# Hybrid decoder step: key steps of the samples moved from the prompt's attention into the projections

## The reference, cut to what matters

```
h = rmsnorm(x);  p = h @ w_in            -> q, k (4 heads x 2 components x 64), v (4 heads x 128), conv input
prompt:  a = softmax(q0.k0) - lam * softmax(q1.k1), causal over 512 keys;  o = a @ v
sample:  the same over 4096 cached keys and the new one;                   o = a @ cached v
x = x + concat(rmsnorm(o), swish(layernorm(causal depthwise conv, 31 taps))) @ w_out
x = x + MoE(rmsnorm(x))                  32 experts, top 4, clamped SwiGLU
```

## Time and profile before

| | |
|---|---|
| median of 3 runs | 1733.65 us (1730.45 to 1736.07) |
| the profiled execution's own time | 1735.41 us |
| its span (first to last instruction) | 1733.7 us |
| busy: PE / DVE / ACT / POOL | 1474.0 / 782.4 / 356.0 / 96.7 us |
| mean granted TensorE clock | 0.903 of full speed |
| DMA | 598.10 MB, mean 345 GB/s |

### The profile page before, as it was taken

The page is one execution under the profiler, slowest core; times in us unless marked ns, Lnnn a source line. Parts: engine busy times, 40 slices in busy tenths (PEclk is TensorE's granted clock), DMA queues, the critical chain, the costliest instruction groups (busy, mean ns, idle before and its releaser), DMA issues.

```text
span 1733.7 us, 32093 instructions
## 1 busy us (share of the span) xinstructions
PE 1474.0 (85%) x11950; PEld 595.0 (34%) x11951; DVE 782.4 (45%) x1160; ACT 356.0 (21%) x822; POOL 96.7 (6%) x173
## 2 busy tenths in 40 slices
PE   3868887779788978899998998999899999899970
PEld 2433333346433354332332332333233332232320
DVE  2789879997786335221332232132132131131326
ACT  3212212222222111111211211212112122121220
POOL 0000010000000000000100000000000000000000
PEclk8989995679898857999999999999899999999995
DMA  9557888988998785598999999999999999999986
GB/s 327 182 187 258 283 295 272 331 279 292 311 301 270 242 352 207 227 392 339 429 420 403 427 417 396 412 418 411 392 421 412 401 428 411 397 428 399 428 351 253
DMA packets 127292, 598.10 MB, mean 345 GB/s; under 512 B 20503, under 2 KB 20517, under 8 KB 102026
## 3 DMA queue, kind: packets, MB, share of 16 engines
q1 hardware_dynamic: 109088, 560.20, 81.9%
q10 hardware_dynamic: 8634, 20.00, 3.4%
q0 software_dynamic: 9504, 17.06, 2.6%
HBM read 589.36 MB, written 25.87 MB: 355 GB/s over the span
## 4 chain that ended last, share of the span: by engine, by line
PE 40%; DMA 19%; DVE 2%; issue 1%; ACT 0%; DVEq 0%; SPq 0%; ACTq 0%
PE bank L1511 25%; DMA wts<-in_w_gate_up 16%; PE bank L1548 8%; PE bank L1530 4%; DMA wts<-in_w_down 3%; PE bank L1501 1%; PE bank L1618 1%; DVE v_ring L2139 1%; PE bank L1559 1%; PE bank L1599 0%; DVE q_b L2139 0%; DMA h_tok<-h_rows,v_tok 0%; ACT k_T L1155 0%; DVEq L2127 0%; ACT k_T L1138 0%
## 5 line engine op out<-in xcount | busy, mean ns | idle before, releaser
L1511 PE MATMUL bank<-wts,h_T 128*32 128x512 f32 x4032 | 443.9, 597 | 9.7 <-DMA wts<-in_w_gate_up 5.2
L2061 DVE TENSOR_SCALAR q_T<-bank 128x512 f32<-128x512 f32 x32 | 22.1, 692 | 636.9 <-PE bank L1511 636.9
L1511 PEld LDWEIGHTS bank<-wts,h_T 128*32 128x32 f32 x4032 | 129.5, 111 | 308.3 <-issue 296.4
L1548 PE MATMUL bank<-wts,k_T 128*32 128x512 f32 x2048 | 228.3, 597 | 8.0 <-issue 4.9
L1530 PE MATMUL bank<-wts,h_T 128*32 128x512 f32 x992 | 132.6, 675 | 52.2 <-DMA wts<-in_w_gate_up 50.4
L1658 DVE TENSOR_TENSOR wts<-wts,q_b 128x1024 f32<-128x1024 f32 x128 | 158.1, 1235 | 23.1 <-DMA wts<-in_cache_k 17.4
L1661 DVE TENSOR_REDUCE sc<-wts 128x16 f32<-128x1024 f32 x128 | 156.2, 1220 | 4.4
L1145 ACT ACTIVATE h_T<-bank 128x512 f32<-128x512 f32 x66 | 35.9, 595 | 573.5 <-PE bank L1501 573.5
L1548 PEld LDWEIGHTS bank<-wts,k_T 128*32 128x32 f32 x2048 | 64.9, 110 | 149.0 <-issue 139.5
L1223 PE MATMUL bank<-wts,h_T 128*8 128x128 f32 (+1 forms) x480 | 92.7, 465 | 12.3 <-ACT h_T L854 6.4
L1155 ACT ACTIVATE k_T<-bank 32x256 f32<-32x256 f32 x256 | 95.7, 374 | 13.6 <-PE bank L1548 10.2
(11 more groups left out here) (330 smaller groups left out, 1375.8 us busy)
## 6 DMA issues: line engine op xcount, KB each, us to landing
wts<-in_w_gate_up SPq DMA_DIRECT2D x126, 2048.0 KB, 15.8
wts<-in_w_down SPq DMA_DIRECT2D x64, 2048.0 KB, 18.3
wts<-in_cache_k SPq DMA_DIRECT2D x256, 256.0 KB, 3.7
v_ring<-in_cache_v SPq DMA_DIRECT2D x160, 256.0 KB, 3.8
wts<-in_cache_v SPq DMA_DIRECT2D x96, 256.0 KB, 3.9
wts<-in_w_in SPq DMA_DIRECT2D x5, 2048.0 KB, 24.1
wts<-y_rows SPq DMA_DIRECT2D x4, 2048.0 KB, 15.1
wts<-in_w_out ACTq DMA_DIRECT2D x8, 512.0 KB, 6.2
```

Of the source, the lines that this page charges most:

```text
L1511: m = nc.tensor.matmul(PS[part][p0:p0 + 32, :], lhs[:, 32 * b:32 * b + 32], rhs[:, part * F + half * 512:part * F + half * 512 + 512], sta ...
L1548: m = nc.tensor.matmul(PS[4][p0:p0 + 32, :], act_T[0][:, k, a0:a0 + 32], chunk[c][:, k, n * 512:(n + 1) * 512], start=(c == 0 and k == 0), ...
```

## The change

Only weights of the schedule change. In the stages of `P 1` (its end) to `P 4` the weight of a key step goes from 1 to `KEYS` = 1.45 per stage. In `Q` it goes from 1 and 0.4 per unit to 0.2 and 0, and in `N` from 1 to 0. The weights of the value steps are the same as before, written out where they were implied. The arithmetic is the same.

```diff
+        KEYS = 1.45
         for s in range(1, TILES + 1):
             if s > 1:
-                plan(("P", s), 1, both=s > 2)
-            plan(("P", s - 1), 1 if s > 1 else 0, both=s > 2)
-            plan(("P", s), 1 if s > 1 else 3, both=s > 2)
+                plan(("P", s), KEYS, values=1 if s > 2 else 0)
+            plan(("P", s - 1), KEYS if s > 1 else 0, values=1 if s > 2 else 0)
+            plan(("P", s), KEYS if s > 1 else 3, values=1 if s > 2 else 0)
...
-            plan(("P", s), 1)
-            plan(("P", s), 1, 1, 1, both=True)
+            plan(("P", s), KEYS)
+            plan(("P", s), *[KEYS] * 3, values=1)
...
         for j in range(UNITS + 3):
             if j < UNITS:
-                plan(("Q", j), 1, both=True)
+                plan(("Q", j), 0.2, values=1)
...
             if j < UNITS:
-                plan(("Q", j), 0.4, values=0.7)
+                plan(("Q", j), 0, values=0.7)
...
             if j > 1 and (j - 1) % H == 0:
-                plan(("N", (j - 1) // H), 1, both=True)
+                plan(("N", (j - 1) // H), 0, values=1)
```

More of the change, by code:

```diff
@@ L224, in hybrid_step @@
         plan(("P", 1), 0)
+        KEYS = 1.45
         for s in range(1, TILES + 1):
             if s > 1:
-                plan(("P", s), 1, both=s > 2)
-            plan(("P", s - 1), 1 if s > 1 else 0, both=s > 2)
-            plan(("P", s), 1 if s > 1 else 3, both=s > 2)
+                plan(("P", s), KEYS, values=1 if s > 2 else 0)
+            plan(("P", s - 1), KEYS if s > 1 else 0, values=1 if s > 2 else 0)
+            plan(("P", s), KEYS if s > 1 else 3, values=1 if s > 2 else 0)
             if s == 1:
                 plan(("C", 0), 2)
-            plan(("P", s), 1, both=s > 1)
-            plan(("P", s - 1), 1, both=s > 1)
+            plan(("P", s), KEYS, values=1 if s > 1 else 0)
+            plan(("P", s - 1), KEYS, values=1 if s > 1 else 0)
             if s == 1:
@@ L239, in hybrid_step @@
                 continue
-            plan(("P", s), 1)
-            plan(("P", s), 1, 1, 1, both=True)
+            plan(("P", s), KEYS)
+            plan(("P", s), *[KEYS] * 3, values=1)
             if s < TILES:
-                plan(("P", s + 1), 1, both=True)
-            plan(("P", s), 2, values=1)
-            plan(("P", s), 1, 1, both=True)
+                plan(("P", s + 1), KEYS, values=1)
+            plan(("P", s), 2 * KEYS, values=1)
+            plan(("P", s), *[KEYS] * 2, values=1)
             if s < TILES:
-                plan(("P", s + 1), 1, both=True)
-        plan(("P", TILES), 1, 1, both=True)
+                plan(("P", s + 1), KEYS, values=1)
+        plan(("P", TILES), *[KEYS] * 2, values=1)
         plan(("Q", 0), 0)
```

## The result

The changed kernel takes 1760.4 us (median of 4 runs, 1758.29 to 1761.47), the kernel before 1733.35 us in the same comparison: 27 us slower, ratio 1.0155 with a 95% interval of 1.0136 to 1.0174. The forecast was slower, at 1751 us. The profiled execution spans 1759.8 us, 26.1 us more than before.

A forecast was written before the change was run, and what follows sets the result against it. DVE was taken to pace both stages. Projections +50.2 - 10 = +40 us, attention -21, edges -1: about +18, rounded to 17, on 1733.7, giving 1751 us; range 1728 to 1770.

The forecast's parts named there:

- the three waits: Projections: DVE's waits for keys, squares and gate, 24.3 us in all, would become about 14.4 us.
- The first wait for squares: Projections, behind the first `pmax`: a second key step fills 2.4 of DVE's 5.9 us wait; 3.5 stay.
- The other waits on TensorE: Projections: DVE's waits for squares (4.2 us) and the gate (3.3 us), from PE being late, would both go.
- the wait for keys: Projections: DVE's 10.9 us of waiting for key loads queued at SP would stay unchanged in total.
- four new waits: Projections, behind `pmax` and `dg`: ring left with two key groups; some 2 us each, 6 to 8 us, partly replacing older waits.
- The chain of a unit: Prompt's attention: maxima, two exponentials, combination, next maxima in sequence; 2.7 to 4.8 us per unit, 60 us for 16.
- The two late key steps: Router stages: two key steps, 4.8 us of DVE, would hide in its 5.79 us wait for `x_in`, costing nothing.
- The balance: Both stages: the change pays only if DVE's waits together stay under 38 us; 55 were expected.
- A (faster): Projections grow 26 to 31 us, attention shrinks 32 to 36 with PE at 2.4 GHz; 1723 to 1732 us; chance 0.22.
- B (work is only shifted): Projections' growth and attention's shrinking differ by under 5 us; 1729 to 1739 us; chance 0.14.
- C (keys run out at SP's stops, +30): Projections: 8 SP stops with 2 to 3 us each give 20 us of key waits; 1764 us; chance 0.14.
- The test by even loading: Projections and attention: DVE at 86% and 92% evens at 88% after two or three key steps; 21 are too many.

The follow-up runs named there:

- the later value loads: Changed kernel, with SP loading value pages two value steps later in its queue: 1747.1 us, ratio 1.0076 to the kernel before.
- the light key steps: Changed kernel, with 21 of 82 key steps in the projections only copying 128x16 elements on DVE, loads kept: 1746.0 us, ratio 1.0069.
- the light key steps in the attention: Kernel before, with the 26 key steps in the prompt's attention only copying 128x16 elements on DVE, loads kept: 1712.4 us, ratio 0.9879.
- the half change: Changed kernel with weights set for 71 key steps up to the projections' end, instead of 61 or 82: 1742.3 us, ratio 1.0050.
- the pair: Changed kernel, with 21 projection key steps reduced to copies and value pages loaded two steps later: 1726.3 us, ratio 0.9959.
- the wider small steps: Changed kernel, with a sample's small softmax steps spread wider and value pages loaded two steps later: 1752.2 us, ratio 1.0120.

## Why the prediction was right, and where its sizes were off

**Projections, +40 expected, +47.4 measured.** The step's frame held: 21 steps of 2.39 us are 50.2 us, and DVE's busy time grew by that; the 50.2 less the 2.3 us by which the three waits fell is the measured growth within half a microsecond. The first wait for squares was to go from 5.9 to 3.5 us and went to 2.7. The other waits on TensorE were to vanish and did. The term that was mis-sized is the wait for keys. It was kept at 10.9 us, on the argument that four new waits of some 2 us would stand partly in place of older ones. It measured 19.3 us at 9 places instead of 5, the one worked out in detail being 2.9 us and the next 4.6. In sum the new waits came on top. This is also over the 9 to 18 us that the prediction gave as a sign of being right, and DVE's 89% is just under its 90%.

**The cause of these waits** was named rightly, SP's value loads ahead of its key loads, and the later value loads show it. What the prediction did not see is that DVE's work and the supply of keys are two bounds of nearly one length. It treated the supply as a surcharge on DVE's work; the light key steps show that the supply, with SP's queue as it stands, holds the stage within 12 us of its new length when DVE's added work is gone.

**Attention, -21 expected, -18.4 measured.** Of the difference 1.0 us is the starting point (272.3 us, where the first maxima begin at 273.34), and the rest is the new length: counted as the prediction counts, 94.5 us where 93 was expected. The chain of a unit and its place were right. In the unit shown the combination begins 3.2 us after the maxima (385.55 to 388.76), where the sum had 1.64 + 1.45 + 0.1; the waits for ACT stand in 13 units. The prediction's frame (55 us of DVE's work out, 21 off the time) was nearly met, and the light key steps in the attention confirm it from the other side. The clock did not rise as the faster rival wanted: 0.71 after 0.68. The sum itself was luckier than its terms. It took TensorE's clock as low for 40% of the time, for which no row stood: a granted clock of 0.68 between the levels 0.50 and 1.00 is 64% of the time at the low one, and the 0.71 measured is 58%. By the same working that is 16 us instead of 11, so other terms were some 3 to 4 us too large, and which ones is not shown. One thing was left out: the longest of these waits, 5.3 us, is one in which ACT's exponentials stood in ACT's queue behind a sample's `ex`, and that behind TensorE's value products.

**The edges.** The two late key steps were to fall before the wait of 5.79 us for `x_in`; that wait is now 1.07 us, 4.7 less:

```profile
578.24 0.69 DVE L1656 TENSOR_TENSOR x_in<-x_in,bank 128x512 f32<-128x512 f32 x1 [1.07 <-DMA x_in<-in_x_prompt]
```

The convolution's first products start at 417.2 us instead of 388.5, 29 us later, where about 406 was expected, and the experts 26.2 us later, so the shift passes on but for 2.8 us.

**The sum.** +18 was expected against +26.1 in the spans. The missing 8 are 7.4 in the projections and 2.6 in the attention, less 2 us at the edges and behind. Both errors made the loss too small, so the direction does not hang on them, but the result lies at the top of the forecast's own band of +7 to +27. The balance that the text gave (the change pays only if DVE's waits stay under 38 us) failed as foreseen. Counted as there, they are 22.0 us in the projections and 39.6 in the attention, 61.6 where 55 was expected.

**The rivals.** A (faster) fell on both legs: the projections grew by 47 us and not 26 to 31, the attention shrank by 18 and not 32 to 36. B (work is only shifted) fell with the result, and the half change loses in proportion. C (keys run out at SP's stops, +30) has the mechanism that made the difference and comes nearest to the measured time (1764 us). It had 13 us more of waits for keys than the forecast, where 8.4 us more were measured; its projections were about 6 us too long, the edges gave back 2 us more than it counted, and the attention 2.6 us less. The Trainium skill ("Perfetto Trace Analysis", section "Optimization Strategy") says that interleaving may help where the most contended engine changes over time. The trace here does not meet that condition: DVE is the busiest engine of both stages, at 86% and 92%. The test by even loading that the prediction drew from it is the prediction's own. It pointed the right way for 21 steps, but it has no place for what a step covers: DVE was fuller in the attention, and a step still was worth less there.

## What to carry to other kernels

Before filler work is moved from one stage to another, price one unit of it in each: here a step of 2.4 us cost 2.3 us where it went, and was worth 0.8 us where it left, where waits for another engine took its place. A queue that issues loads in program order is part of the schedule: denser consumption between two of its stops can empty a ring that was deep enough before. Where two bounds lie close together, removing either alone can show little (9.9 and 11.9 us here, 34.4 for the pair, and in the kernel before nothing for one of them), so an edit without effect does not clear its suspect; try the pair.

## What the runs showed that was not expected

The same edit in SP's queue is worth 13 us at 82 key steps in the projections (1760.4 to 1747.1) and nothing at 61 (ratio 0.9997). The attention takes the same 94 us with DVE busy 50.1 us at a DMA share of 1.02 and with 54.9 us at 0.71. And the value pages, loaded two steps later, made TensorE wait 3.7 us for them in the kernel before and 12.2 us in the changed kernel with the wider small steps, so the cure has a price of its own.
